# Hybrid encoder layer on one core: gate products split over attention, recurrence under the U products, softmax sums from a block of ones

## The reference, cut to what matters

```python
z = rms_norm(x, g_mix_norm) @ w_in                 # [q latent 256 | kv latent 128 | rope key 32 | u | gate_a | gate_b]
# branch A: latent attention, 16 heads, QK-norm, causal in chunks of 64
p = softmax(where(visible, s * scale, -inf)); attn = p @ v
# branch B: width-4 causal conv of u, then the RG-LRU
r, i = sigmoid(u_c @ w_rg + b_rg), sigmoid(u_c @ w_ig + b_ig)
a = exp(-8 * r * softplus(-lam)); bt = sqrt(1 - a * a) * i * u_c
h[t] = a[t] * h[t-1] + bt[t]
mixed = sigmoid(gate_a) * attn + sigmoid(gate_b) * h
x = x + mixed @ w_out
x = x + (silu(conv3(gate)) * conv3(val)) @ w_down  # up = rms_norm(x) @ w_up
```

## Time and profile before

| | |
|---|---|
| three runs | 945.20, 946.52, 2200.45 us, median 946.52 |
| profiled execution | 945.21 us, of which the span from first to last instruction is 943.3 us |
| PE busy | 899.4 us (95%), 6689 instructions |
| PEld | 847.8 us (90%) |
| DVE busy | 604.8 us (64%) |
| ACT busy | 347.5 us (37%) |
| POOL busy | 238.3 us (25%) |
| mean granted TensorE clock | 0.982 of full speed |

### The profile page before, as it was taken

One profiled execution on the slowest core, in us unless ns is written; L12 is line 12 of the kernel. 1 busy time (PEld: TensorE's weight loads), 2 busy tenths in 40 slices (PEclk: granted clock), 3 DMA queues, 4 the chain that ended last, 5 costly groups with the idle time before them and its releaser, 6 DMA issues.

```text
span 943.3 us, 18508 instructions
## 1 busy us (share of the span) xinstructions
PE 899.4 (95%) x6689; PEld 847.8 (90%) x6689; DVE 604.8 (64%) x1182; ACT 347.5 (37%) x619; POOL 238.3 (25%) x278
## 2 busy tenths in 40 slices
PE   5999999998799999998999999999999999999998
PEld 5899999987577887776799999999999999999998
DVE  4378634686789888897544488777778777322221
ACT  6331455364344444442423533333333332112111
POOL 4000233462333221331012233333333333201000
PEclk8999999999899999997999999999999999999999
DMA  8333323322000000010003232233332222233321
GB/s 256 79 84 76 97 78 82 77 73 46 15 7 10 14 14 14 20 27 1 1 23 90 67 110 78 81 88 89 89 89 82 78 85 84 84 97 104 98 70 36
DMA packets 114630, 63.55 MB, mean 67 GB/s; under 512 B 7836, under 2 KB 113054, under 8 KB 114588
## 3 DMA queue, kind: packets, MB, share of 16 engines
q1 hardware_dynamic: 112396, 59.17, 22.4%
q0 software_dynamic: 2192, 3.81, 1.8%
HBM read 59.85 MB, written 2.70 MB: 66 GB/s over the span
## 4 chain that ended last, share of the span: by engine, by line
PE 86%; DVE 6%; issue 4%; ACT 2%; POOL 1%; SPq 1%; DMA 0%; DVEq 0%; ACTq 0%; POOLq 0%
PE PS L1141 61%; PE PS L1354 4%; PE PS L1338 4%; PE PS L1319 3%; PE PS L1176 3%; PE PS L1265 2%; PE PS L1308 2%; PE PS L1214 2%; PE PS L1261 1%; PE PS L1362 1%; PE PS L1292 1%; PE PS L1283 1%; DVE small L1010 1%; DVE w_lo L773 0%; PE PS L1325 0%
## 5 line engine op out<-in xcount | busy, mean ns | idle before, releaser
L541 ACT ACTIVATE w_hi<-w_raw 128x1024 fp32r<-128x1024 f32 (+2 forms) x104 | 107.6, 1035 | 368.7 <-PE PS L1141 354.4
L773 DVE TENSOR_TENSOR w_lo<-w_raw,w_hi 128x1024 fp32r<-128x1024 f32 (+2 forms) x104 | 128.1, 1231 | 122.8 <-ACT w_hi L541 122.6
L1141 PE MATMUL PS<-x2h,w_hi 128*128 128x274 f32 x704 | 147.7, 291 | 1.1 <-DVE w_lo L773 1.1
L1141 PE MATMUL PS<-x2h,w_lo 128*128 128x274 f32 x704 | 146.9, 290 | 0.0
L1141 PE MATMUL PS<-x2l,w_hi 128*128 128x274 f32 x704 | 146.9, 290 | 0.0
L1141 PEld LDWEIGHTS PS<-x2h,w_hi 128*128 128x128 f32 x704 | 111.9, 189 | 1.4 <-issue 1.3
L1141 PEld LDWEIGHTS PS<-x2l,w_hi 128*128 128x128 f32 x704 | 112.0, 189 | 0.0
L1141 PEld LDWEIGHTS PS<-x2h,w_lo 128*128 128x128 f32 x704 | 111.4, 189 | 0.0
L1141 PE MATMUL PS<-xnh,w_hi 128*128 128x274 f32 x384 | 83.3, 299 | 4.4 <-DVE w_lo L773 2.3
L1141 PE MATMUL PS<-xnl,w_hi 128*128 128x274 f32 x384 | 81.7, 295 | 0.0
L1141 PE MATMUL PS<-xnh,w_lo 128*128 128x274 f32 x384 | 81.0, 293 | 0.0
(11 more groups left out here) (254 smaller groups left out, 1706.6 us busy)
## 6 DMA issues: line engine op xcount, KB each, us to landing
w_raw<-in_w_up_dram SPq DMA_DIRECT2D x44, 512.0 KB, 3.8
w_raw<-in_w_in_dram SPq DMA_DIRECT2D x24, 512.0 KB, 3.9
w_raw<-in_w_down_dram SPq DMA_DIRECT2D x16, 512.0 KB, 3.7
w_raw<-in_w_out_dram SPq DMA_DIRECT2D x8, 512.0 KB, 4.1
w_raw<-in_w_down_dram SPq DMA_DIRECT2D x8, 384.0 KB, 3.9
xnat<-in_x_prompt_dram SPq DMA_DIRECT2D x4, 512.0 KB, 5.0
w_raw<-in_w_in_dram SPq DMA_DIRECT2D x4, 416.0 KB, 4.7
wq<-in_w_q_b_dram SPq DMA_DIRECT2D x8, 192.0 KB, 2.5
```

What stands on the lines that cost most here:

```text
L541: nc.scalar.activation(hi[:, slot % 2, 0:n], raw[:, slot % 4, 0:n], ACT.Copy).then_inc(s_hi, 1)
L773: tt(lo[:, slot % 2, 0:n], raw[:, slot % 4, 0:n], hi[:, slot % 2, 0:n].bitcast(F32), ALU.subtract).then_inc(s_lo, 1)
L1141: last = mm(PS[:, 2 * rank + j, 0:HT], w[:, slot % 2, cols], x[:, k0 + k, j * HT:(j + 1) * HT], start=(k0 + k == 0 and first), stop=(k0 + ...
```

## The change

- Items. The 24 items of `w_in` become a first list of 12 (gate_a and gate_b block 0, the eight of u, gate_a and gate_b block 1), and 12 more (blocks 2 to 7) that are multiplied inside attention, as halves of 24 matmuls over 274 columns: pairs 0 to 4 take two items, pairs 5 and 6 one. The first pair of output items moves its splits into pairs 5 and 6.
- Latents. Norms, latent tiles and columns of the cache move behind the first item, on DVE ahead of the split of item 6. The transposes move behind items 0, 2, 3.
- Recurrence. `lru` follows items 4 to 10; exps, squares, roots and scans of blocks 0 to 3 go behind items 8 and 9, of blocks 4 to 7 behind the last. The first convolution tap moves to ACT. sigmoid of the gates becomes 1 + tanh(x/2), with the half taken in at the end.
- Softmax. Probabilities stay undivided. V gets a block of 64 ones between the two heads' values, and each value matmul takes 128 weight columns, values and ones, so half of its output rows hold the sum of the row's exponentials, 64 times over. ACT copies the sums (`head_sums`), DVE takes the reciprocal of 128x548 per pair in two halves, POOL multiplies and adds the recurrence (`mix`), ACT and DVE form hi and lo. `row_inverse`, the diagonal and ACT's row sums go; `transpose_probs` is now a true transpose. Score banks go from three to two.
- Output. Items 0 and 1 are multiplied for channel blocks 0 to 6 first, then both for block 7, so that they end together.
- SP's queue is written out: weights of the pairs and items interleaved. All loops over U stage, prelude and attention are unrolled.

```diff
+FIRST = [("A", 0), ("B", 0)] + [("U", n) for n in range(KD)] + [("A", 1), ("B", 1)]
+def fills(p):
+    return [I_G + 2 * p, I_G + 2 * p + 1] if p < 5 else [I_G + 5 + p] if p < 7 else []
...
# DVE, first list
+            for g, (kind, n) in enumerate(FIRST):
+                dve.wait_ge(s_used, I_IN + g + 1)
+                dst = U[:, n, LEAD:] if kind == "U" else gate(kind, n)
+                tt(halves(dst), pair(g), halves(rsT[:, :]), ALU.mult).then_inc(s_free, 1)
+                if g == 0:
+                    latent_norms()
+                    for t in range(NTT):
+                        latent_tile(t)
+                    past_columns()
+                if g in (2, 3):
+                    for t in (range(4) if g == 2 else range(4, 5)):
+                        latent_columns(t)
+                if kind == "U":
+                    conv(n)
+                split_item(I_IN + g + 2)
+                if g == 8:
+                    for q in range(4):
+                        lru_m2(q)
+                if g == 9:
+                    for q in range(4):
+                        recurrence(q)
+                if g == 10:
+                    key_sums(0)
+                    query_sums(0)
+                    normalise_keys(0)
+                    normalise_queries(0)
+            for q in range(4, KD):
+                lru_m2(q)
+            dve.wait_ge(s_rope4, 48)
+            for v in range(5):
+                columns(0, v, 2 + v % 2)
+            for q in range(4, KD):
+                recurrence(q)
...
# DVE, attention, by step n
+                    if n == 0 and following:
+                        normalise_keys(p + 1)
+                    if n == 1:
+                        if p:
+                            sums_inverse(p - 1, 0)
+                        if following:
+                            normalise_queries(p + 1)
+                    if n == 2:
+                        if p:
+                            sums_inverse(p - 1, 1)
+                        if 1 <= p <= 5:
+                            split_item(17 + 2 * p)
+                    if n == 3 and following:
+                        columns(p + 1, 0, 0)
+                        columns(p + 1, 1, 1)
+                        gate_half(gate_items[0], 0)
...
+            def sums_inverse(p, j):
+                cols = slice(j * HT, (j + 1) * HT)
+                dve.wait_ge(s_sum, 2 * p + 2)
+                dve.wait_ge(s_o, 3 * p + 3)
+                ins = nc.vector.reciprocal(sums[:, cols], sums[:, cols])
+                if j:
+                    ins.then_inc(s_ri, 1)
...
+            def gated_values(p, h):
+                g_p = gate("A", p)[rows(h), 0:SEQ]
+                dve.wait_ge(s_gt, gate_count("A", p))
+                dve.wait_ge(s_pv, 9 * p + 4 * (h + 1))
+                stt(g_p, g_p, 1.0, values_bank(h)[rows(h), :], ALU.add, ALU.mult).then_inc(s_o, 1)
+            def gated_sample(p):
+                dve.wait_ge(s_pv, 9 * p + 9)
+                for h in range(2):
+                    bank = PS[:, 6 + p % 2, SEQ - R2 + h * DEC:SEQ - R2 + (h + 1) * DEC]
+                    g_p = gate("A", p)[rows(h), S0:]
+                    stt(g_p, g_p, 1.0, bank[rows(h), :], ALU.add, ALU.mult)
+                    last = nc.vector.tensor_copy(sums[rows(h), S0:], bank[rows(1 - h), :])
+                last.then_inc(s_o, 1)
...
# PE, first list
+            for g, (kind, n) in enumerate(FIRST):
+                if g == 1:
+                    pe.wait_ge(s_nat, 1)
+                if g >= 2:
+                    pe.wait_ge(s_free, g - 1)
...
+                product(xnh, xnl, g % 2, [(I_IN + g, I_IN + g, 0, KD)])
...
+                if 4 <= g < 11:
+                    lru(g - 4)
+                if g == 10:
+                    pe.wait_ge(s_free, 10)
+                    keys_queries(0, 0, 2)
+                    keys_queries(0, 1, 3)
+                    pe.wait_ge(s_free, 11)
+                    keys_queries(0, 2, 0)
+                    lru(7)
+                    keys_queries(0, 3, 1)
+                    for u in (4, 5):
+                        pe.wait_ge(s_kqf, u - 1)
+                        keys_queries(0, u, u - 4)
...
# ACT, first list
+            for g, (kind, n) in enumerate(FIRST):
+                if kind == "U":
+                    first_tap(g, n)
+                split_item(I_IN + g + 2)
+                if kind != "U":
+                    act.wait_ge(s_free, g + 1)
+                    gate_tanh(gate(kind, n))
+                if g == 8:
+                    lru_exps(0)
+                if g == 9:
+                    lru_mults(0)
+                if 4 <= g < 11:
+                    lru_gates(g - 4)
...
# PE, attention
-                    last = mm(bank[:, a * P:(a + 1) * P], Pn[:, n % 3, a * P:(a + 1) * P], dg[:, n % 3, :], start=True, stop=True)
+                    last = nc.tensor.transpose(bank[:, a * P:(a + 1) * P], Pn[:, n % 3, a * P:(a + 1) * P], ident[:, :])
-                        last = mm(PS[h * VD:(h + 1) * VD, 3, t * P:(t + 1) * P], V[:, par, a, h, :], PT[:, b, a * P:(a + 1) * P],
-                                  start=(a == 0), stop=(a == t))
+                        last = mm(values_bank(h)[:, t * P:(t + 1) * P], V[:, par, a, h:h + 2, :].rearrange("p h n -> p (h n)"),
+                                  PT[:, b, a * P:(a + 1) * P], start=(a == 0), stop=(a == t))
...
+                    if following and n == 3:
+                        for v in range(2):
...
+                            transpose_kq(p + 1, v, v)
+                        pe.wait_ge(s_trf, 5 * (p + 1) + 1)
+                        gate_half(first, 0)
+                    if following and n == 4:
+                        pe.wait_ge(s_trf, 5 * (p + 1) + 2)
+                        gate_half(first, 1)
+                    if second and n == 7:
+                        pe.wait_ge(s_trf, 5 * (p + 1) + 5)
+                        gate_half(second, 0)
+                    if second and n == 8:
+                        pe.wait_ge(s_vf, 3 * (p + 1) + 1)
+                        gate_half(second, 1)
...
# POOL, between prelude and attention
+            for n in range(4, KD):
+                lru_input(n)
+            squares_keys(1)
+            squares_queries(1)
+            pool.wait_ge(s_rec, KD)
+            nc.gpsimd.memset(V[:, :, :, 1, :], 1.0).then_inc(s_clear, 1)
...
# PE
+            pe.wait_ge(s_clear, 2)
+            for p in range(NP_):
+                attend(p)
...
-            for r in range(KD):
-                pe.wait_ge(s_free, G_OUT + r - 1)
-                product(mxh, mxl, r % 2, [(I_OUT + r, r, 0, KD)], (s_ml, 0) if r == 0 else None)
+            for r in range(2):
...
+                output_product(r, 0, KD - 1)
+            for r in range(2):
+                output_product(r, KD - 1, 1).then_inc(s_used, 1)
+            for r in range(2, KD):
+                pe.wait_ge(s_free, G_OUT + r - 1)
+                product(mxh, mxl, r % 2, [(I_OUT + r, r, 0, KD)])
```

More of the change, by code:

```diff
@@ L369, in _ @@
+            for t in range(I_OUT + 6, I_UP):
+                w_out_item(t)
             with sp.Fori(0, NU // 4) as it:
@@ L661, in exps, with evacuate_v @@
+            def evacuate_v(q, u, bank):
+                if u == 0 and q >= 2:
+                    act.wait_ge(s_pv, q * 9 - 9)
+                act.wait_ge(s_v, q * 3 + (u + 1))
+                tiles, p0 = (4, 0) if u < 2 else (1, LASTP)
+                dst = V[p0:, q % 2, 4 * u:4 * u + tiles, 0:3:2, :]
+                nc.scalar.activation(dst, PS[p0:, bank, 0:tiles * P].rearrange("p (t h n) -> p t h n", h=2, n=VD), ACT.Copy).then_inc(s_vf, 1)
+            def exps(p, n):
                 act.wait_ge(s_mx, p * 9 + (n + 1))
-                after(act, s_pt, p * 9 + (n - 2 if reused else max(n - 2, 0)))
@@ L715, in _ @@
+            for u in range(4):
+                evacuate_kq(1, u, 4 + u)
+            lru_mults(1)
+            for u in range(4, 6):
+                evacuate_kq(1, u, u - 4)
+            act.wait_ge(s_rec, KD)
+            for u in range(3):
+                evacuate_v(0, u, (0, 1, 5)[u])
+            exps(0, 0)
+            for p in range(NP_):
+                attend(p)
+            mixed_hi(7)
             with act.Fori(0, 2) as it:
@@ L990, in row_max @@
                 dve.wait_ge(s_s, p * 9 + (n + 1))
-                bank, sm = PS[:, SB[n % 3], :], small[:, 4 + n % 3, :]
+                bank, sm = score_bank(p, n), small[:, 4 + n % 3, :]
                 if n < 8:
@@ L1066, in _ @@
-            attend(6, 0)
-            attend(7, 1)
+            dve.wait_ge(s_rec, KD)
+            for p in range(NP_):
+                attend(p)
+            sums_inverse(7, 0)
+            sums_inverse(7, 1)
+            dve.wait_ge(s_ri, NP_)
+            o_p, h_p = gate("A", 7), U[:, 7, LEAD:]
+            dve.wait_ge(s_o, 3 * NP_)
+            link(tt(o_p, o_p, sums[:, :], ALU.mult))
+            dve.wait_ge(s_hb, NP_)
+            tt(h_p, h_p, o_p, ALU.add).then_inc(s_mix, 1)
```

(26 more changed lines are left out.)

919 lines of the change are left out of this document (492 added, 427 removed).

## The result

| | before | after |
|---|---|---|
| median of four runs | 945.9 us (945.20, 945.29, 946.52 and 2200.45) | 998.67 us (997.7 to 998.93) |
| profiled execution, span | 945.2, 943.3 us | 998.5, 996.7 us |
| mean granted TensorE clock | 0.982 | 0.943 |

The ratio of after to before is **1.0559**, with a 95% interval of 1.0538 to 1.0579; the one run of 2200.45 us is not in it. The change is 5.6% slower. The sign of the forecast holds; 974 us was 25 too low, and 998.7 lies 5 above 994, the upper end of the range.

A forecast was written before the change was run, and what follows sets the result against it. PE was taken as the main bound (86% of the chain), with DVE's fixed-order queue second. From 945.2 us, +18.5 for U stage and prelude, +5 attention and +5.3 output items gave 974 us, range 921 to 994.

The forecast's parts named there:

- The start and the first products: Prelude: first item starts at 43.2, saving 3.9 us; third product waits 6.6 for its split weights, 8.4 with the clock.
- Waits under list items 8 to 11: Prelude: PE waits 1.7, 2.0, 3.5 and 1.8 us for ACT and DVE, plus 1.8 for the clock: 10.8.
- The tail: Prelude's end: norms, rotation, copies, four recurrences and pair 1's sums; attention starts 32 us after item 11.
- DVE's side: Attention pairs: 1.85 us per reciprocal half, first KT copy at 12.5 us, bank 0 free at 14.0, PE waiting 3.4.
- the sum of a pair: Attention, pairs 1 to 4: 44.1 us each against 41.7, so +2.4 each, +10 in all.
- The clock, 1.8 once a pair: Attention, behind step 3's wait: half-speed TensorE clock after the pause costs 1.8 us more than the pause.
- The sample values, +0.5: Attention: 20 short sample value matmuls with 128 weight columns cost +0.5 us a pair, +4 in all.
- The transposes, -2.4: Attention: transposes replacing diagonal matmuls save 22 x 0.11 = 2.4 us of PE per pair, 19 in all.
- Output items: After attention: item 2 waits 3.5 us for its w_lo behind items 0 and 1, plus 1.8 clock: +5.3.
- Transposes let the clock fall: Rival, attention: half the 10 us before step 3 at 1.2 GHz, 4 us more in 6 pairs, 998; 0.1 with others.
- Cheap reciprocal: Rival, attention: 0.45 us a reciprocal half, PE hardly waits and the clock holds, 28 off, 946 us; chance 0.2.
- PE is the only bound: Rival, prelude and attention: DVE's queue gives way, new attention waits and half the prelude's vanish, 921 us; chance 0.18.

The follow-up runs named there:

- experiment 2: After with DVE's queue reordered: reciprocals and second gate item's rounding behind the copies into KT, next item's rounding in step 7, block B first; 951.71 us.
- experiment 8: Full probability blocks multiplied by the identity instead of transposed: 955.26 us on the kernel with DVE reordering, early prelude roundings and early output item 0; 1007.89 us on after.
- 10: Combined edits with after's last pair, early exponential table and regrouped recurrences: 934.82 us; additionally step 3's first half product behind its transposes and value matmuls: 926.67 us.
- experiment 1: After with the two wide reciprocals of each pair replaced by a multiply by 1.0 of the same size, leaving out the division; 967.66 us.
- The kernel of 926.67 us: Combined-edit kernel of 934.82 us, with the first half product of step 3 moved behind that step's transposes and value matmuls; 926.67 us, ratio 0.9797.

## Why the prediction was wrong

**The start and the first products held.** Product 1 starts at 43.24 (43.2 forecast). The third was to wait for a w_lo finished at 63.0, and starts at 63.33, at half clock for the next 5.6 us.

**Waits under list items 8 to 11 held in their sum, the clock there did not.** PE waits 1.67, 4.53, 2.06 and 1.51 us, in sum 9.8, where the prediction had 1.7, 2.0, 3.5 and 1.8, in sum 9.0. The second, for ACT, was 2.5 too short and the third, for DVE, 1.4 too long; that the sum fits is in part luck. And I took 1.8 for the clock. The window from 140.0 to 166.4 has 21.07 us of busy PE at 0.74; 21.07 x 0.26 is an estimate of 5.5 us lost, 3.7 more. With 0.8 of waits, and 0.3 of wait and some 1.0 of clock at the third product, this is about why item 11 ends at 166.3 instead of 160.8.

**The tail was 34.5 instead of 32, by several small terms.** POOL's rotation ends at 182.3, 16.0 us behind item 11 (15 forecast), and the last copy into QT at 185.9, another 0.7 late. The four recurrences take 9.5 us for 10.0, and this is luck. The 2.5 us of the earlier trace rows run from the first copy of a round to the round's second scan; the scan before them took 1.30 us, with POOL idle. Here three recurrences take 1.65 us each, and the first 4.6, beside POOL's products. The two row maxima (0.6) were missing from the sum. Attention started 8.0 us later than forecast.

**In the pairs DVE's side held to a tenth.** The reciprocal takes 1.85 us, as taken. The first copy into KT starts 12.4 us into the pair (12.5 forecast) and bank 0 is free at 13.9 (14.0). PE has its transposes done at 9.7, not 10.6, so the wait is 4.28 instead of 3.4. In step 7 it is 2.28 instead of 1.7.

**The step that failed is the sum of a pair: "29.4 - 2.4 + 12.3 + 0.5 + 3.4 + 1.8 + 1.7 - 2.6 (old waits now filled) = 44.1".** Four terms were mis-sized, the clock most of all; the same price of 1.8 was too low in the prelude.
- The clock, 1.8 once a pair. In the 47.5-us pairs PE is busy for 40.94 us, where 37.1 do with the clock at 1.00 (experiment 2): 3.8 lost; in the 44.6-us pairs 1.0. Pair 5 is busy for 34.95 us against 31.27 in experiment 2: 3.7 lost. The price came from one pause, and by that row's records it is 1.5: 12 of 28 missing, 0.128 each. The trace of before had dearer pauses, in its pair 6 above all:

```profile
427.20:458.50 31.30, 27.10 (x172) 20.70 (x172) 21.34 (x65) 10.46 (x33) 3.86 (x12) 0.84 0.00 1
```

- The waits, 1.5 us a pair too short.
- The sample values, +0.5. The group's row, 1.15 us in the same view of before, is now 2.32, so +1.2, just above the upper end that was named, 1.1:

```profile
288.74 2.32 PE L1552 MATMUL PS<-PT,V 128*128 128x32 f32 x20
```

- The transposes, -2.4: they are worth 1.9 (experiment 8). A pair has 19 of them before and 42 after by the trace; the prediction's 17 and 40 leave out two small ones.

Against these stand more old waits filled than the 2.6: some 3.9, an estimate from what is left over in either kind of pair. That the short pairs end at 44.6, near the forecast, is luck: the errors cancel there. The long ones end at 47.5, pair 5 at 41.5 (37.5 forecast), pair 6 at 37.5 (35.4), pair 0 at 42.7 (41.4), pair 7 at 18.5 (17.4). Attention lost 15.7 us more than forecast. With the prelude's 8.0 and 0.8 behind attention this is the 24.5 by which the sum missed.

**Output items held**: +6.1 for +5.3, with a pause of 3.46 us (3.5 forecast) and half clock behind it.

**The rivals.** *Transposes let the clock fall* named 998 us, nearly the result, for a reason that the runs speak against: the clock fell behind pauses, and with matmuls in place of the transposes the four pairs have 0.93, no better than 0.89 and 0.96 by turns. By the rule of "TensorE: Matmul & The Clock Gate", section "Part 4: PE-mode transpose", in the Trainium skill, pairs with 42 transposes should have been at risk; the trace does not agree, with 1.00 in the pairs of experiments 2 and 10.

*Cheap reciprocal* priced its gain well, 28 us, where experiment 1 gained 31. Its 946 was off because the 974 that it started from was.

*PE is the only bound* named 921 us (its terms add up to 920) and the condition that bank 0 is free when PE comes. In after it is not: it is free at 13.9 us into the pair, and PE has its transposes done at 9.7. The kernel of 926.67 us comes near the number but is no test of its sum: its attention starts at 189.0, 14.7 us later than the 174.3 of before, which this rival's sum does not hold, and its pairs of 37.3 us make up for it.

## What to carry to other kernels

Work moved beside another stage is paid for by the queue that both share: ask for each copy that frees a buffer what stands ahead of it on its engine and could stand behind it. Here the same operations, but for one small exponential, gave 998.7 or 926.7 us by their order. When you price a pause of TensorE, give the clock behind it a range of its own, and sum it over all the pauses, not one a pair.
